# Head norms of a two-block transformer: the sum of squares in two reduced fp32 matmuls in place of one in plain fp32

## The chip, the core and the metric

The kernel runs on one core of one Trainium2 chip. The metric is the device time of one execution in microseconds (us); the time of a version is the median of its runs. Engines: PE is TensorE (matmuls; PEld is its loading of weights), DVE is VectorE, ACT is ScalarE, POOL is GpSimd, SP issues the DMAs.

## What is computed

A sequence of 512 tokens of width 1024 goes through two transformer blocks. The first has a stick-breaking attention, a forgetting attention ("fox") and an attention over 256 memory tokens; the second has a gated delta rule (the GDN stage, 8 heads of width 128), a banded attention and a cross attention. What matters here are the norms over a head:

```python
def rmsnorm(x, g):
    xf = x.astype(jnp.float32)
    y = xf * lax.rsqrt(jnp.mean(xf * xf, axis=-1, keepdims=True) + EPS)
    return (y * g.astype(jnp.float32)).astype(x.dtype)
...
        fq = rmsnorm(to_heads(fx_q, FOX_HEADS, HD), g_fox_q[l])
        fk = rmsnorm(to_heads(fx_k, FOX_HEADS, HD), g_fox_k[l])
...
        mq = rmsnorm(to_heads(m_q, MEM_HEADS, MEM_HD), g_mem_q[l])
        mk = rmsnorm(to_heads(mk, MEM_HEADS, MEM_HD), g_mem_k[l])
...
def _l2norm(x):
    return x * lax.rsqrt(jnp.sum(x * x, axis=-1, keepdims=True) + EPS)
...
    q = _l2norm(_to_chunks(q.astype(f32), A_HEADS, A_DK)) * (A_DK ** -0.5)
    k = _l2norm(_to_chunks(k.astype(f32), A_HEADS, A_DK))
...
        oa = rmsnorm_2(oa, head_norm[l]) * jax.nn.silu(za.reshape(b, s, A_HEADS, A_DV))
```

## The kernel before

Activations lie transposed: 128 features on the partitions, the 512 tokens (256 for the memory) along the row. A projection (`product`, L983) takes 128 output features at a time and eight blocks of 128 input features. Weights and activations are each split into a rounded high part and the rest, so each block costs three matmuls in the reduced fp32 format (f32r in the code, fp32r in the profile): `hh` by `whi` (L995), `hl` by `whi` (L997) and `hh` by `wlo` (L1001). The weights come in units of eight blocks, 512 KB: SP loads a unit into `stage`, ACT rounds it into `whi` (L1413), and DVE (L1778) or POOL (L2238) subtracts to get `wlo`, in stages that `lo_engine` sets. POOL does it in the fox stage and in the GDN stage, DVE in the memory projections.

A norm over a head is four steps of `Schedule.norm` (L384), laid out over several turns of the schedule so that other work lies between them: `hn_sq`, ACT squares the rows (L1478, `norm_square`); then an empty turn; `hn_mm`, PE sums over the features with one plain fp32 matmul against a matrix of ones, or of two blocks of ones for heads of 64 (`head_norm`, L1017, recorded as L950), and ACT takes Ln (L1451) and Exp (L1453) of the sum; `hn_out`, DVE multiplies the rows by it (L1883, recorded as L1781). There are 40 such norms: 4 over the memory keys with 256 columns, 8 for q and k of the fox heads, 4 for the memory queries (these 12 in the fox stage), and in the GDN stage 16 for q and k (`l2q`, `l2k`) and 8 for the output of a head (`oa`), all with 512 columns. The squares of the `oa` norm lie in buffers of the head's cell (`cu`, `cwt`), those of all others in `sqb0`, so an `oa` norm and an `l2k` norm can be under way together.

Each engine works its own list of steps in order, and the list is one order for all: the generators of `Schedule` are mixed (`mix`, `pipe`, `par`), `settle` (L891) sets the banks and what must be free before a step, and each engine's program runs through that one list and issues what is its own. Nothing overtakes on an engine: an instruction that waits holds up all behind it. In the fox stage the projections of the next pair and the norms are interleaved with softmax blocks: DVE finds a maximum (L1932), ACT takes the exponential (L1560, L1575), DVE scales by the sum (L1943, L1958), PE transposes (L953), ACT copies back (L1567, L1582) and PE multiplies by the values. In the GDN stage PE alternates between small 64x64 matmuls that invert a triangle (tiles in `ya`, with DVE between them), the scan of the head before (`cu`, `cs`, `cuu`), and projections of the head after.

The square step on ACT and the matmul of a norm on PE before:

```python
    def norm_square(o):
        wait(o.raw_ref)
        free(o.u_sq)
        act.activation(o.sq, o.raw, ACT.Square).then_inc(*up("hn_sq", o.no))
...
    def head_norm(o):
        pe.wait_ge(*at("hn_sq", o.no))
        free(o.u_bank)
        mm(bank[o.u_bank.bank][:, 0:o.n], o.ones, o.sq, True, True).then_inc(*up("pe_hn", o.no))
```

Of the kernel before, what the change touches and what calls it, by code (L numbers as in the profile page):

```python
# [8 lines left out]
F32 = mybir.dt.float32  # L9
# [7 lines left out]
T = 512  # L17
# [117 lines left out]
class Kernel:  # L135
# [43 lines left out]
    def allocate(self):  # L179
# [3 lines left out]
        self.R = sb("rr", [128, T])  # L183
        self.vecs, self.cft = sb("vecs", [128, NVEC]), sb("cft", [128, NCF])
        self.cbt = sb("cbt", [128, NCB], BF16)
        self.acc = sb("acc", [128, T])
# [23 lines left out]
    def allocate_block1(self):  # L210
# [18 lines left out]
        self.fb = [sb(f"fb{i}", [128, T]) for i in range(4)]  # L229
        self.lf, self.fr, self.lfe = sb("lf", [128, 4, 8]), sb("fr", [128, T]), sb("lfe", [128, 4, 8])  # L230
        self.fxst = [sb(f"fxst{i}", [128, 4]) for i in two]
# [92 lines left out]
class Norm:  # L324
# [13 lines left out]
    u_bank: Use  # L338
    u_out: Use


# [22 lines left out]
class Schedule:  # L364
# [19 lines left out]
    def norm(self, no, out, u_out, raw, raw_ref, ones, scale, gain, n=T, bank="b7", work=None):  # L384
        k = self.k
        sq, r, psq, pr = work or (k.sqb[0][:, 0:n], k.sqb[1][:, 0:n], "sqb0", "sqb1")
        o = Norm(no, out, raw, ones, scale, gain, n, raw_ref, sq, r, Use(psq, [("pe_hn", no)]), Use(pr, [("hn_out", no)]),
                 Use(bank, [("hn_ln", no)]), u_out)
        yield [st("hn_sq", o, o.u_sq)]
        yield []  # L390
        yield [st("hn_mm", o, o.u_bank, o.u_r)]
        yield [st("hn_out", o, *([u_out] if u_out else []))]
# [61 lines left out]
    def mem_kv(self, w, name, raw, nt, mk, mv, gain):  # L454
        items = []
        src = ("mem", w)
        for i in range(2 * nt):
# [8 lines left out]
            elif gain:  # L466
                u = Use(place, [("hn_out", no)])
                g = self.gemm(name, 128 * i, range(8), src, "copy", u, ev, n=NM, out=r[:])
                items.append((g, self.norm(no, mk[:, i, :], None, r[:], ("act_ev", key), self.k.cf("ones"), 1 / 128, self.k.vec(gain), n=NM)))
            else:  # L470
# [49 lines left out]
    def fox_proj(self, p):  # L520
        k, s = self.k, p % 2
        d = self.done2("fox", p)
        pair = k.cf("pair")
        return [self.normed(("fq", p), k.q[s][:], Use(f"q{s}", d), 0, 1536 + 128 * p, pair, 1 / 64, k.vec("g_fox_q")),
# [72 lines left out]
    def block1(self):  # L597
# [14 lines left out]
        def mem_proj(i):  # L612
            return [self.normed(("mq", i), self.mq[i], Use(f"mq{i}", []), i % 2, 3080 + 128 * i, k.cf("ones"), 1 / 128, k.vec("g_mem_q"))]

# [57 lines left out]
    def gdn_proj(self, h):  # L672
# [38 lines left out]
        def unit():  # L711
            yield from silus(*((n, h, k.g3[s][n], ("conv", (n, h))) for n in "qk"))
            for n, g in (("q", 128 ** -0.5), ("k", 1.0)):
                b = k.g3[s][n][:]
                yield from self.norm(("l2" + n, h), b, None, b, ("silu", (n, h)), k.cf("ones"), 1.0, g)

# [40 lines left out]
    def gdn_scan(self, h):  # L757
# [4 lines left out]
        for n in range(8):  # L762
# [4 lines left out]
            if n < 7:  # L767
# [4 lines left out]
        o = k.goT  # L772
        yield from self.norm(("oa", h), o, None, o, ("gc_o", h), k.cf("ones"), 1 / 128, k.vec("head_norm_2"),
                             bank="b6", work=(k.gcell[c]["u"][:], k.gcell[c]["wt"][:], f"cu{c}", f"cwt{c}"))
# [168 lines left out]
def tensor_program(k, pe):  # L943
# [73 lines left out]
    def head_norm(o):  # L1017
        pe.wait_ge(*at("hn_sq", o.no))
        free(o.u_bank)
        mm(bank[o.u_bank.bank][:, 0:o.n], o.ones, o.sq, True, True).then_inc(*up("pe_hn", o.no))  # L1020

# [369 lines left out]
def scalar_program(k, act):  # L1391
# [83 lines left out]
    def norm_square(o):  # L1475
        wait(o.raw_ref)
        free(o.u_sq)
        act.activation(o.sq, o.raw, ACT.Square).then_inc(*up("hn_sq", o.no))  # L1478

    def norm_rsqrt(o):  # L1480
# [197 lines left out]
    for kind, a in k.order:  # L1678
# [10 lines left out]
        elif kind == "tables":  # L1689
            tables()  # L1690
        elif kind == "nsq":
            mem_square(*a)
# [68 lines left out]
def vector_program(k, dve):  # L1761
# [104 lines left out]
    def mem_norm(w, i, gain):  # L1866
# [7 lines left out]
        if i:  # L1874
            hi, lo = (k.mh1, k.mh2)[w - 1]
            dve.wait_ge(*at("sp_hi", (("mem", w), i - 1)))
            tt(lo[:, i - 1, :], tmp[(i - 1) % 2][:], hi[:, i - 1, :].bitcast(F32), ALU.subtract).then_inc(*up("mem_lo", (w, i - 1)))

    def head_norm(o):
# [256 lines left out]
    for kind, a in k.order:  # L2136
# [16 lines left out]
        elif kind == "nout":  # L2153
            mem_norm(*a)
        elif kind == "hn_out":
            head_norm(a)
# [326 lines left out]
```

## Time and profile before

| what | value |
|---|---|
| median of 3 runs | 2376.72 us (2376.33 to 2380.16) |
| the profiled execution, its own time | 2377.33 us |
| its span in the trace | 2375.6 us |
| mean granted TensorE clock over the span | 0.986 |
| instructions in the trace | 32440 |
| busy: DVE, ACT, POOL | 1194.5, 888.9, 432.2 us |

The span is what the trace covers; the profiled execution's own time lies 1.7 us above it. A row of the groups has the line, the engine, the operation, output and inputs by the program's names without buffer numbers, shapes, and a count. A row of the timeline has the start, the duration (of all that are merged into it), the same names, and in brackets how long the engine had been idle before it and what ended that. The end of a matmul is modelled; the distance between the starts of neighbouring matmuls is what the engine really took.

### The profile page before, as it was taken

The page shows a single profiled execution, that of the slowest core. Times are in us where ns is not written, and L with a number is a line of the kernel's source. Part 1 is how long each engine was busy: PE and PEld are TensorE (multiplying, and loading weights), DVE is VectorE, ACT ScalarE, POOL GpSimd, SP SyncE. Part 2 cuts the span into 40 slices and gives each one's busy share as a digit, 9 for nine tenths or more (in the row PEclk, how much of TensorE's full clock was granted, in tenths as well). Part 3 has the DMA queues.
Part 4 walks back from the last instruction along what each step waited for, and adds up shares of the span by engine and source line. Part 5 has one row for each costly group of instructions (what it writes and reads, how often), then busy time and mean ns, then how long its engine had stood idle before and what let it go on. Part 6 is the DMA issues. An engine that isn't in the chain of part 4 may idle for free.

```text
span 2375.6 us, 32440 instructions
## 1 busy us (share of the span) xinstructions
PE 2276.6 (96%) x12924; PEld 1817.5 (77%) x12924; DVE 1194.5 (50%) x1956; ACT 888.9 (37%) x1420; POOL 432.2 (18%) x293
## 2 busy tenths in 40 slices
PE   7999999999999999899999999999999999999997
PEld 5766777888888888677777778777687988888885
DVE  5444454445443444667777522666445445444443
ACT  5444564223322223334333342444434434222222
POOL 1222221001110112434444242000011001101001
PEclk8999999999999999999999999999999999999998
DMA  5213212333333323211121123222133512333332
GB/s 179 80 37 98 63 48 87 90 100 94 98 94 102 98 89 98 86 50 46 56 70 37 36 60 109 81 72 89 54 98 107 157 38 90 98 98 98 98 98 71
DMA packets 58358, 198.94 MB, mean 84 GB/s; under 512 B 6736, under 2 KB 6864, under 8 KB 57952
## 3 DMA queue, kind: packets, MB, share of 16 engines
q1 hardware_dynamic: 58208, 196.86, 26.4%
q8 instruction: 104, 1.70, 0.3%
q14 instruction: 46, 0.38, 0.1%
HBM read 194.67 MB, written 2.16 MB: 83 GB/s over the span
## 4 chain that ended last, share of the span: by engine, by line
PE 50%; DVE 5%; ACT 2%; issue 2%; POOL 1%; DMA 0%; SPq 0%; DVEq 0%; ACTq 0%; POOLq 0%
PE bank L995 14%; PE bank L1001 13%; PE bank L997 13%; PE bank L950 9%; PE bank L953 2%; DVE gv L1781 1%; DVE gq L1781 1%; DVE ya L1778 0%; ACT whi L1413 0%; ACT bdpt L1567 0%; DVE gk L1781 0%; DVE gq L2041 0%; POOL wlo L2238 0%; DVE wlo L1778 0%; ACT cwt L1451 0%
## 5 line engine op out<-in xcount | busy, mean ns | idle before, releaser
L995 PE MATMUL bank<-hh,whi 128*128 128x512 f32 x1680 | 688.3, 410 | 11.5 <-ACT whi L1413 11.5
L1001 PE MATMUL bank<-hh,wlo 128*128 128x512 f32 x1680 | 659.3, 392 | 2.1 <-DVE wlo L1778 1.6
L997 PE MATMUL bank<-hl,whi 128*128 128x512 f32 x1680 | 657.9, 392 | 0.0
L1778 DVE TENSOR_TENSOR wlo<-stage,whi 128x1024 fp32r<-128x1024 f32 x260 | 343.3, 1320 | 295.0 <-ACT whi L1413 294.6
L1413 ACT ACTIVATE whi<-stage 128x1024 fp32r<-128x1024 f32 x340 | 357.4, 1051 | 344.4 <-PE bank L1001 332.5
L995 PEld LDWEIGHTS bank<-hh,whi 128*128 128x128 f32 x1680 | 317.5, 189 | 81.0 <-issue 9.1
L1001 PEld LDWEIGHTS bank<-hh,wlo 128*128 128x128 f32 x1680 | 317.0, 189 | 73.4 <-DVE wlo L1778 3.7
L997 PEld LDWEIGHTS bank<-hl,whi 128*128 128x128 f32 x1680 | 317.9, 189 | 62.8 <-issue 3.6
L2238 POOL TENSOR_TENSOR wlo<-stage,whi 128x1024 fp32r<-128x1024 f32 x80 | 193.9, 2425 | 426.9 <-ACT whi L1413 426.9
L1778 DVE TENSOR_TENSOR x<-bank,x 128x512 f32<-128x512 f32 x80 | 55.3, 692 | 154.2 <-PE bank L1001 154.2
L2238 POOL TENSOR_TENSOR acc<-acc,sqb 128x512 f32<-128x512 f32 x42 | 55.7, 1325 | 325.2 <-ACT sqb L1426 324.6
L995 PE MATMUL bank<-u1h,whi 128*128 128x512 f32 x256 | 99.6, 389 | 0.0
L997 PE MATMUL bank<-u1l,whi 128*128 128x512 f32 x256 | 99.6, 389 | 0.0
L1001 PE MATMUL bank<-u1h,wlo 128*128 128x512 f32 x256 | 99.6, 389 | 0.0
L950 PEld LDWEIGHTS bank<-ya 64*64 64x64 f32 (+1 forms) x2048 | 73.8, 139 | 26.7 <-issue 22.4
L2238 POOL TENSOR_TENSOR u1l<-f1t,u1h 128x512 fp32r<-128x512 f32 x32 | 41.4, 1293 | 265.1 <-ACT u1h L1509 265.1
L950 PE MATMUL bank<-ya 64*64 64x64 f32 (+2 forms) x2048 | 87.3, 231 | 0.0
L2238 POOL TENSOR_TENSOR u2l<-f2s,u2h 128x512 fp32r<-128x512 f32 x22 | 28.5, 1296 | 299.7 <-ACT u2h L1518 299.7
L997 PE MATMUL bank<-u2l,whi 128*128 128x512 f32 x176 | 68.6, 390 | 0.0
L1001 PE MATMUL bank<-u2h,wlo 128*128 128x512 f32 x176 | 68.5, 389 | 0.0
L995 PE MATMUL bank<-u2h,whi 128*128 128x512 f32 x176 | 68.5, 389 | 0.0
L1509 ACT ACTIVATE u1h<-f1t 128x512 fp32r<-128x512 f32 x32 | 20.2, 632 | 126.6 <-DVE f1t L1778 126.6
(363 smaller groups left out, 3471.1 us busy)
## 6 DMA issues: line engine op xcount, KB each, us to landing
stage<-in_wall SPq DMA_DIRECT2D x340, 512.0 KB, 3.5
band<-in_toep SPq DMA_DIRECT2D x16, 256.0 KB, 4.4
x<-in_xT SPq DMA_DIRECT2D x8, 256.0 KB, 5.6
fb<-rowsf SPq DMA_DIRECT2D x8, 256.0 KB, 3.8
gbc<-rows SPq DMA_DIRECT2D x8, 256.0 KB, 3.2
gbc<-rowsc SPq DMA_DIRECT2D x16, 128.0 KB, 3.7
out_y<-fout SPq DMA_DIRECT2D x8, 256.0 KB, 2.2
memx<-in_memT SPq DMA_DIRECT2D x1, 1024.0 KB, 8.8
```

Of the source, the lines that this page charges most:

```text
L950: return pe.matmul(out, w, r, start=start, stop=stop, skip_group_check=True)
L953: return pe.transpose(out, in_, k.cf("ident"))
L995: pe.matmul(o, wh, hi, start=j == 0, stop=False)
L997: pe.matmul(o, wh, lo, start=False, stop=False)
L1001: i = pe.matmul(o, wl, hi, start=False, stop=end)
L1413: act.activation(k.whi[u % NSPLIT][:], k.stage[u % NSTAGE][:], ACT.Copy).then_inc(*up("whi", u))
L1509: act.activation(k.u1[0][:, a["t"] % 16, :], a["b"][:], ACT.Copy).then_inc(*up("sp_hi", ("u1", a["t"])))
L1778: return dve.tensor_tensor(out, a, b, op)
L1781: return dve.scalar_tensor_tensor(out=out, in0=a, scalar=s, in1=b, op0=op0, op1=op1)
L2238: return pool.tensor_tensor(out, a, b, op)
```

## The change

The squares are split like the weights. ACT squares as before, then waits for its own square and copies it, rounded, into `sqh`; DVE subtracts and leaves the rest in `sql`; PE sums both with two matmuls in reduced fp32 into the same bank, against copies of the matrices of ones in that format, which ACT makes once near the start. `sqh` and `sql` exist once: the next norm's copy waits for the second matmul of the norm before (`pe_hn`). The buffer of the plain squares is free once `sql` is written. To make room, the row buffer `fr` of the forgetting attention now lies in `acc`.

```diff
@@ -182,6 +182,8 @@
+        self.sqh, self.sql = sb("sqh", [128, T], F32R), sb("sql", [128, T], F32R)
+        self.onesr = {"ones": sb("onesr", [128, 128], F32R), "pair": sb("pairr", [128, 128], F32R)}
@@ -227,7 +229,7 @@
-        self.lf, self.fr, self.lfe = sb("lf", [128, 4, 8]), sb("fr", [128, T]), sb("lfe", [128, 4, 8])
+        self.lf, self.fr, self.lfe = sb("lf", [128, 4, 8]), self.acc, sb("lfe", [128, 4, 8])
@@ -384,9 +387,9 @@ Schedule.norm
-        o = Norm(no, out, raw, ones, scale, gain, n, raw_ref, sq, r, Use(psq, [("pe_hn", no)]), Use(pr, [("hn_out", no)]),
-                 Use(bank, [("hn_ln", no)]), u_out)
-        yield [st("hn_sq", o, o.u_sq)]
+        o = Norm(no, out, raw, ones, scale, gain, n, raw_ref, sq, r, Use(psq, [("hn_lo", no)]), Use(pr, [("hn_out", no)]),
+                 Use(bank, [("hn_ln", no)]), u_out, Use("sqhl", [("pe_hn", no)]))
+        yield [st("hn_sq", o, o.u_sq, o.u_hl)]
...
@@ -1015,9 +1018,13 @@ PE
     def head_norm(o):
-        pe.wait_ge(*at("hn_sq", o.no))
+        wait(("onesr", 0))
+        pe.wait_ge(*at("hn_hi", o.no))
         free(o.u_bank)
-        mm(bank[o.u_bank.bank][:, 0:o.n], o.ones, o.sq, True, True).then_inc(*up("pe_hn", o.no))
+        out = bank[o.u_bank.bank][:, 0:o.n]
+        mm(out, o.ones, k.sqh[:, 0:o.n], True, False)
+        pe.wait_ge(*at("hn_lo", o.no))
+        mm(out, o.ones, k.sql[:, 0:o.n], False, True).then_inc(*up("pe_hn", o.no))
@@ -1476,6 +1483,14 @@ ACT
         act.activation(o.sq, o.raw, ACT.Square).then_inc(*up("hn_sq", o.no))
+        free(o.u_hl)
+        act.wait_ge(*at("hn_sq", o.no))
+        act.activation(k.sqh[:, 0:o.n], o.sq, ACT.Copy).then_inc(*up("hn_hi", o.no))
+
+    def ones():
+        act.wait_ge(*at("ld_cf", 0))
+        for name, t in k.onesr.items():
+            act.activation(t[:], k.cf(name), ACT.Copy).then_inc(*up("onesr", 0))
@@ -1876,6 +1893,10 @@ DVE
+    def square_lo(o):
+        dve.wait_ge(*at("hn_hi", o.no))
+        tt(k.sql[:, 0:o.n], o.sq, k.sqh[:, 0:o.n].bitcast(F32), ALU.subtract).then_inc(*up("hn_lo", o.no))
```

`square_lo` is issued at the step `hn_sq` of the list, `ones` at the step `consts`, right before the weight units of the memory keys. All norms now take their ones from `k.onesr`.

How the lists of the engines change, at two places. First ACT in the GDN stage, at a head's `oa` norm (squares in `cu`) and the `l2k` norm of the head after (squares of `gk` in `sqb`). Before:

```order
L1453 ACTIVATE sqb<-sqb 128x512 [waits hn_ln]
L1478 ACTIVATE cu<-ya 128x512 [waits gc_u,gc_s,pe_po,gc_o]
L1478 ACTIVATE sqb<-gk 128x512 [waits pe_hn,silu]
L1451 ACTIVATE cwt<-bank,eps 128x512 [waits pe_hn]
L1453 ACTIVATE cwt<-cwt 128x512 [waits hn_ln]
L1451 ACTIVATE sqb<-bank,eps 128x512 [waits pe_hn,hn_out]
```

and of the change:

```order
L1460 ACTIVATE sqb<-sqb 128x512 [waits hn_ln]
L1485 ACTIVATE cu<-ya 128x512 [waits gc_u,gc_s,pe_po,gc_o]
L1488 ACTIVATE sqh<-cu 128x512 [waits hn_sq,pe_hn]
L1485 ACTIVATE sqb<-gk 128x512 [waits hn_lo,silu]
L1488 ACTIVATE sqh<-sqb 128x512 [waits hn_sq,pe_hn]
L1458 ACTIVATE cwt<-bank,eps 128x512 [waits pe_hn]
L1460 ACTIVATE cwt<-cwt 128x512 [waits hn_ln]
L1458 ACTIVATE sqb<-bank,eps 128x512 [waits pe_hn,hn_out]
```

The second copy into `sqh` stands ahead of the Ln of the first norm and waits for PE to be done with the first norm's two matmuls. On DVE at the same place, of the change, with buffer numbers:

```order
L1795 TENSOR_TENSOR ya<-bank3,cft 128x256 [waits pe_P,pe_Y]
L1795 TENSOR_TENSOR sql<-cu1,sqh 128x512 [waits hn_hi]
L1798 SCALAR_TENSOR_TENSOR gq1<-gq1,sqb1 128x512 [waits hn_r]
L1798 SCALAR_TENSOR_TENSOR gz_0<-bank0,rr 128x512 [waits pe_w,gs_oz]
L1795 TENSOR_TENSOR sql<-sqb0,sqh 128x512 [waits hn_hi]
L1795 TENSOR_TENSOR ya<-ya,bank4 128x256 [waits pe_Y]
```

Both subtractions are new; the second stands ahead of the last correction of `ya` that the small matmuls of the inverse wait for. Second DVE in the fox stage, at the norm of q of the fourth pair (`mmst` and `sbW` belong to a memory block, `fxzb`, `fxst` and `sbA` to a fox block). Of the change:

```order
L1971 TENSOR_SCALAR mmst<-mmst 128x2 [waits sm_mx]
L1795 TENSOR_TENSOR sql<-sqb0,sqh 128x512 [waits hn_hi]
L1953 ISA fxzb0,fxst0<-bank2,fb0 128x384 [waits pe_s,sm_n,sm_p]
L1953 ISA fxst0 128x1
L1956 TENSOR_SCALAR fxst0<-fxst0 128x1 [waits sm_mx]
L1953 ISA fxzb1,fxst1<-bank3,fb1 128x384 [waits pe_s,sm_n,sm_p]
L1953 ISA fxst1 128x1
L1956 TENSOR_SCALAR fxst1<-fxst1 128x1 [waits sm_mx]
L1975 RECIPROCAL mmst<-mmst 128x2 [waits sm_p]
L1979 TENSOR_SCALAR sbW0<-sbW0,mmst 128x256 [waits sm_rc]
```

Before, the first row is followed at once by the `fxzb0` row; the subtraction now stands between them.

## Rows read from the trace of the kernel before

**Rows 1.** The page, its first section: the busiest engine

```profile
PE 2276.6 (96%) x12924; PEld 1817.5 (77%) x12924; DVE 1194.5 (50%) x1956; ACT 888.9 (37%) x1420; POOL 432.2 (18%) x293
```

**Rows 2.** Windows: us, PE, PEld, DVE, ACT, POOL busy (count), clock, DMA share, GB/s

```profile
183.00:335.00 152.00, 147.17 (x786) 106.42 (x785) 71.97 (x190) 79.24 (x177) 36.92 (x16) 1.00 0.23 74
955.00:1420.00 465.00, 432.38 (x3988) 338.01 (x3986) 289.67 (x473) 186.78 (x261) 183.75 (x119) 0.98 0.17 54
```

**Rows 3.** Timeline of PE around one norm of the fox stage

```profile
199.16 0.39 PE L1001 MATMUL bank<-hh,wlo 128*128 128x512 f32 x1
199.39 1.02 PE L950 MATMUL bank<-sqb,cft 128*128 128x512 f32 x2
...
200.48 0.40 PE L997 MATMUL bank<-hl,whi 128*128 128x512 f32 x1
```

**Rows 4.** The squares, line L1478: ns min/median/max, first and last start

```profile
L1478 ACT ACTIVATE sqb<-qr x12: 613/616/632, 183.1 to 321.5; 128x512 f32<-128x512 f32 x12
L1478 ACT ACTIVATE sqb<-gq x8: 611/612/617, 971.0 to 1314.3; 128x512 f32<-128x512 f32 x8
...
L1478 ACT ACTIVATE cu<-ya x8: 615/616/631, 1069.0 to 1408.7; 128x512 f32<-128x512 f32 x8
L1478 ACT ACTIVATE sqb<-mraw x4: 402/406/407, 42.5 to 58.4; 128x256 f32<-128x256 f32 x4
```

**Rows 5.** The nearest copies and subtractions, by line and by tile

```profile
L1676 ACT ACTIVATE oah<-ya x8: 613/641/644, 1075.3 to 1416.5; 128x512 fp32r<-128x512 f32 x8
L1778 DVE TENSOR_TENSOR cqd<-gq,ya x8: 678/680/684, 995.2 to 1343.8; 128x512 f32<-128x512 f32 x8
L1778 DVE TENSOR_TENSOR oml<-nm1tmp,omh x8: 412/426/1518, 27.7 to 39.9; 128x256 fp32r<-128x256 f32 x8
L1778 DVE TENSOR_TENSOR sbA<-sbA x16: 292/412/2383, 86.2 to 191.1; 128x128 f32<-128x128 f32 x8, 128x256 f32<-128x256 f32 x8
```

**Rows 6.** Timeline, where the new copies of the ones come in

```profile
42.13 0.58 PE L1001 MATMUL bank<-omh,wlo 128*128 128x256 f32 x1 [0.45 <-DVE wlo L1778]
```

**Rows 7.** Timeline, the second norm of the memory keys

```profile
51.82 0.41 ACT L1478 ACTIVATE sqb<-mraw 128x256 f32<-128x256 f32 x1
...
51.95 1.23 DVE L1778 TENSOR_TENSOR wlo<-stage,whi 128x1024 fp32r<-128x1024 f32 x1 [1.93 <-ACT whi L1413]
...
52.33 0.65 PE L950 MATMUL bank<-sqb,cft 128*128 128x256 f32 x2
...
53.08 0.47 ACT L1451 ACTIVATE sqb<-bank,eps 128x256 f32<-128x256 f32 x1 [0.85 <-PE bank L950]
```

**Rows 8.** Timeline of the fox stage at the norm of q of the fourth pair

```profile
309.45 0.56 DVE L1932 CUSTOM_DVE_ANT_0 fxzb<-bank,fb 128x384 f32<-128x384 f32 x1
...
310.94 0.63 ACT L1478 ACTIVATE sqb<-qr 128x512 f32<-128x512 f32 x1
...
311.13 2.41 POOL L2238 TENSOR_TENSOR wlo<-stage,whi 128x1024 fp32r<-128x1024 f32 x1 [12.54 <-ACT whi L1413]
...
313.84 0.63 PE L953 MATMUL bank<-cft,sbW 128*128 128x128 f32 x4
```

**Rows 9.** Timeline of the GDN stage, a cluster of two norms and what follows

```profile
1119.59 0.62 ACT L1478 ACTIVATE cu<-ya 128x512 f32<-128x512 f32 x1
...
1120.97 1.13 PE L950 MATMUL bank<-cu,cft 128*128 128x512 f32 x2
...
1124.76 1.50 DVE L1781 SCALAR_TENSOR_TENSOR gk<-gk,sqb 128x512 f32<-128x512 f32 x1 [0.49 <-ACT sqb L1453]
...
1126.69 5.39 DVE L1781 SCALAR_TENSOR_TENSOR gv<-cx,vecs,gv 128x512 f32<-128x512 f32 x3
...
1132.46 0.68 PE L950 MATMUL bank<-cft,ya 64*64 64x64 f32 x16 [2.27 <-DVE ya L1778]
```

**Rows 10.** Timeline of PE at the start of the GDN stage

```profile
971.63 2.08 PE L950 MATMUL bank<-sqb,cft 128*128 128x512 f32 x2 [3.06 <-ACT sqb L1478]
...
989.67 0.59 PE L950 MATMUL bank<-cft,ya 64*64 64x64 f32 x6 [4.50 <-DVE ya L1778]
```

More of the change, by code:

```diff
@@ L339 @@
     u_out: Use
+    u_hl: Use
 @dataclass(eq=False)
@@ L468, in mem_kv @@
                 g = self.gemm(name, 128 * i, range(8), src, "copy", u, ev, n=NM, out=r[:])
-                items.append((g, self.norm(no, mk[:, i, :], None, r[:], ("act_ev", key), self.k.cf("ones"), 1 / 128, self.k.vec(gain), n=NM)))
+                items.append((g, self.norm(no, mk[:, i, :], None, r[:], ("act_ev", key), self.k.onesr["ones"][:], 1 / 128, self.k.vec(gain), n=NM)))
             else:
@@ L522, in fox_proj @@
         d = self.done2("fox", p)
-        pair = k.cf("pair")
+        pair = k.onesr["pair"][:]
         return [self.normed(("fq", p), k.q[s][:], Use(f"q{s}", d), 0, 1536 + 128 * p, pair, 1 / 64, k.vec("g_fox_q")),
@@ L612, in mem_proj @@
         def mem_proj(i):
-            return [self.normed(("mq", i), self.mq[i], Use(f"mq{i}", []), i % 2, 3080 + 128 * i, k.cf("ones"), 1 / 128, k.vec("g_mem_q"))]
+            return [self.normed(("mq", i), self.mq[i], Use(f"mq{i}", []), i % 2, 3080 + 128 * i, k.onesr["ones"][:], 1 / 128, k.vec("g_mem_q"))]
         def blocks(a, b):
@@ L714, in unit @@
                 b = k.g3[s][n][:]
-                yield from self.norm(("l2" + n, h), b, None, b, ("silu", (n, h)), k.cf("ones"), 1.0, g)
+                yield from self.norm(("l2" + n, h), b, None, b, ("silu", (n, h)), k.onesr["ones"][:], 1.0, g)
         def chain():
@@ L772, in gdn_scan @@
         o = k.goT
-        yield from self.norm(("oa", h), o, None, o, ("gc_o", h), k.cf("ones"), 1 / 128, k.vec("head_norm_2"),
+        yield from self.norm(("oa", h), o, None, o, ("gc_o", h), k.onesr["ones"][:], 1 / 128, k.vec("head_norm_2"),
                              bank="b6", work=(k.gcell[c]["u"][:], k.gcell[c]["wt"][:], f"cu{c}", f"cwt{c}"))
@@ L1690, in scalar_program @@
             tables()
+        elif kind == "consts":
+            ones()
         elif kind == "nsq":
@@ L2154, in vector_program @@
             mem_norm(*a)
+        elif kind == "hn_sq":
+            square_lo(a)
         elif kind == "hn_out":
```

## The prediction, written before the change was run

> **What bounds the kernel now.** I read the page first: PE is busy 96% of the span, 2276.6 of 2375.6 us [rows 1]. So PE time that is taken away is time saved, unless PE then waits. The windows say where it already waits: in the fox stage it is idle 4.8 of 152 us, in the GDN stage 32.6 of 465 us [rows 2]. The timelines at the norms decide the rest. For each of the 40 norms I asked three things: when does ACT end the square, when does PE come to the norm's matmul, and what do DVE and POOL do in between. The new work lies exactly in that gap.
>
> **What PE saves.** Matmuls of a projection start about 0.23 us apart. From the L1001 at 199.16 to the L997 at 200.48 lie 1.32 us, in which PE does that L1001, the norm and one L995: two normal steps of 0.23 leave 0.86 us for the plain fp32 matmul, recorded as two passes [rows 3]. Two matmuls in reduced fp32 are two normal steps, 0.46 us. That is 0.40 us saved for each of the 36 norms with 512 columns (12 + 8 + 8, and 8 more of `gk` that look like those of `gq`) [rows 4], and about 0.2 for the 4 with 256. All of it together: 36 x 0.40 + 4 x 0.2 = 15.2 us. This is the most that can be won.
>
> **What is added on the way from square to sum.** Before, the path was the square alone. Now it is: a copy on ACT, 0.64 us by the copy `oah<-ya`; a subtraction on DVE, 0.68 us by `cqd<-gq,ya`, 0.43 for 256 columns by `oml` [rows 5]. PE can issue the second matmul about 1.4 us after the square ends if DVE is free and in turn. Two things make it later. DVE works in order, so the subtraction waits for what stands before it and holds what stands behind. And it reads two operands from SBUF: subtractions of that sort (`sbA<-sbA`) usually take 0.3 to 0.4 us but up to 2.38 us [rows 5], and the three `gv` multiplications took 5.39 us while POOL was busy, where three of 0.7 would be 2.1 [rows 9]. I read this as follows: such an instruction of DVE doesn't move while POOL's runs, and ends some 0.55 us after it.
> The Trainium skill says the same in SBUF — State Buffer, section "Who interferes with whom": a DVE instruction with two SBUF inputs and a GpSimd instruction that reads SBUF exclude each other for the whole instruction. By that rule the fox term below is what I give; without it the subtraction there would end 1.2 us earlier and the sum would be about 2.4 us lower.
>
> **Ones.** Two copies of 128x128 on ACT stand right before a weight split that PE is already waiting for through DVE's `wlo` [rows 6]. No row shows that size; between 0 and two of the 0.64 us for four times the columns, I take 0.25 each, as half the size of the 0.4 us operations with 256 columns (estimate): **+0.5**, bounds 0 and 1.3.
>
> **Memory keys, 4 norms.** The first has 4 us of room and what follows waits for something else: 0. In the other three the square (51.82 to 52.23) ends as PE arrives at 52.33. The copy ends near 52.63, but DVE is in `wlo` until 53.18 and the subtraction stands behind it: 53.2 to 53.63, second matmul at 53.7. Before, the passes ended 0.65 us after their start and the Ln came 0.1 later, at 53.08; a single cheaper matmul ends some 0.28 after its start (estimate), so the Ln comes near 54.08 [rows 7]. Ln, Exp, the eviction, the weight split and the next square follow each other on ACT without a gap, so the 1.0 us doesn't come back: 3 x 1.0 = **+3.0** (bounds 2.4 and 3.6).
>
> **Fox stage, 12 norms.** The slack between square and PE is 2.7 to 6.4 us, so the matmul itself is in time everywhere, even with POOL's 2.4 us in the way: 12 x -0.40 = -4.8. But the subtraction also delays the softmax chain behind it on DVE. In eight of the twelve PE doesn't need that chain soon. The dearest is the q norm of the fourth pair: DVE did the maximum `fxzb` at 309.45, before the square (310.94 to 311.57). Now the subtraction stands in front and waits for the copy (312.2), then for POOL (until 313.54), and ends at 314.1. The two maxima (0.56 and, by my estimate, 0.15 for their small operations), and a reciprocal with a scaling (0.5 together, estimate) come after: `sbW` is ready at 316.1 where PE wanted it at 313.84 [rows 8]: +2.3. Three more places of the same kind, with less of a delay, give by the same working 0.4, 0.9 and 0.8, and one more costs the 0.4 that it saves. Sum: -4.8 + 2.3 + 2.1 + 0.4 = **0.0**, bounds -4.8 (the chain has slack I don't see) and +4.
>
> **GDN stage, 24 norms.** At the start PE waits 3.06 us for the square and then does the fp32 matmul at the low level of the clock in 2.08 us [rows 10]; the copy and subtraction add 1.35, the cheaper matmuls take about that much off: 0. Its k norm saves 0.4 ahead of a wait of 4.5 us on DVE [rows 10]: 0. The next two norms (second head): -0.4 and -0.1. Then six times the cluster of rows 9. The q norm ahead of it saves 0.4, and all that follows starts 0.4 earlier: square of `oa` at 19.19 (+1100), copy to 20.45, subtraction 20.55 to 21.24, second matmul near 21.4, its sum known at 21.85. Only then the second copy may overwrite `sqh`: to 22.47. DVE meanwhile has `gq` and `gz` behind the first subtraction, 0.68 each as in rows 5, and is free at 22.6; second subtraction to 23.3, second matmul 23.4. So the Exp of the k norm ends, and `gk` can start, at 25.2 instead of 24.76: +0.45. PE's inverse starts near 23.8, 0.9 later than before. But neither sets the pace: PE stands 2.27 us at 1132.46 waiting for DVE, and DVE is held by alternating with POOL in the `gv` multiplications (5.39 us) [rows 9]. POOL's chain starts only 0.15 to 0.2 later, so I take +0.2 a head, net of what the q norm saves; the bounds are -0.4 (all hidden) and +0.9 (PE's delay passes through). 6 x 0.2 = +1.2. The last two `oa` norms: -0.4 and, where the weight split stands behind the copy, +0.6. Sum of the stage: **+0.9**, bounds -2.7 and +5.1.
>
> **Sum:** 0.5 + 3.0 + 0.0 + 0.9 = **+4.4 us**, on the profiled execution's own 2377.33 us: 2381.7. The median of the runs is 0.6 us lower than that execution; what I left at nothing (ACT's extra 0.64 us in front of exponentials, 12 times in the fox stage) can only add. I forecast **2382 us**: PE's saving of 15 us is real, and is spent on waits for the new chain. About 0.2% (4.8 us) is what a measurement can tell from no change, and the forecast lies on that edge.
>
> **The rivals.**
> 1. *The waits are covered* (faster). Where DVE's delay meets slack in both softmax and inverse, the fox stage gives -4.8 and the GDN stage -2.7: with 3.5 for the start that is -4.0, or 2373, just inside the bound; each us that the memory keys hide as well takes it below, down to -15.2 or 2362. For it: the slack of 3 us and more at most norms, PE's share of 96%. Against it: rows 7, where nothing lies between square and matmul. Chance 0.13 for over 0.2% faster.
> 2. *One buffer for two norms* (slower). `sqh` is shared, so at the six clusters the second norm can't start before the first is summed, and DVE holds the subtraction in front of the correction of `ya` that PE's inverse needs. If that delay of 0.9 us passes through instead of vanishing in the wait of 2.27 us, it is +4.2 over my sum; with the fox stage at its upper bound, +4. Then 2386 to 2390. It decides as soon as PE's wait at rows 9 is used up, or POOL's chain moves by as much as ACT's. Chance 0.43 for over 0.2% slower, the upper half of my own range included.
> 3. *The matmuls don't get cheaper*: were each of the two to cost what half the plain one does, 0.43, nothing would be saved and the time would be 2397. The projections' step of 0.23 us in the same format speaks against it; 0.02, inside the chance of slower.
>
> **How the numbers follow.** The forecast's own neighbourhood, 2373 to 2381.5, has 0.44 (same), rival 1 has 0.13 (faster), the rest 0.43 (slower). The range takes in the bounds of the fox and GDN stages, which I don't expect to fall on the same side both: 2372 to 2391.
>
> **What would show it.** In the profile after: the pair of matmuls 0.46 us apart from start to the next projection where they don't wait; in the memory keys a wait of PE for DVE's `sql` of about 1 us, three times; near 313.8 a wait of PE for `sbW` of 2 us; DVE rows `sql` of up to 3 us in the fox stage where POOL runs; at a cluster a wait of about 0.4 us before each second matmul, and the distance between clusters, 50.6 us before (from 1069.0 [rows 4] to 1119.59 [rows 9]), at 50.8. It would be wrong if the distance is under 50.3 or over 51.4, or if the stretch from 183 to 335 gets shorter by more than 3 us.

## The result and the profile after

| | before | after |
|---|---|---|
| median | 2376.39 us (2375.06 to 2380.16, 12 runs) | 2382.76 us (2376.44 to 2384.6, 12 runs) |
| span of the profiled execution | 2375.6 us | 2382.8 us |
| mean granted clock over it | 0.986 | 0.983 |

The ratio of after to before is 1.002 with the interval [1.001, 1.0029]: slower by 6.4 us. The forecast was 2382, so the number was right. Two things were missing from its reasons, the granted clock in the fox stage and what ACT's copy does in front of an exponential, and the first of them is what most of the experiments are about. The profiled execution of the changed kernel is the slowest of its twelve runs (2384.60 us); three of the twelve took 2376.4 to 2377.1 us, at a mean clock of 0.986 to 0.987.

The page after, its first section, and below the dots the new groups from the list of all groups by shape (busy us and mean ns, then idle time before them and what ended it):

```profile
PE 2275.8 (96%) x12924; PEld 1823.4 (77%) x12924; DVE 1220.8 (51%) x1996; ACT 913.2 (38%) x1462; POOL 435.8 (18%) x293
...
L1795 DVE TENSOR_TENSOR sql<-sqb,sqh 128x512 fp32r<-128x512 f32 x28 | 29.3, 1048 | 23.1 <-ACT sqh L1488 22.5
L1488 ACT ACTIVATE sqh<-sqb 128x512 fp32r<-128x512 f32 x28 | 17.7, 631 | 6.8 <-PE bank L953 4.8
L953 PE MATMUL bank<-sql,onesr 128*128 128x512 f32 x28 | 13.2, 471 | 3.3 <-DVE sql L1795 3.3
L953 PE MATMUL bank<-sqh,onesr 128*128 128x512 f32 x28 | 13.1, 469 | 8.1 <-ACT sqh L1488 8.1
```

Against [rows 1], PE's busy time is the same within 1 us although the plain fp32 passes are gone; DVE has 26 us more and ACT 24 us more. A part of PE's saving must have gone back into PE being slower, and the windows say where (us, PE, PEld, DVE, ACT, POOL busy, clock, DMA share, GB/s):

```profile
183.00:335.00 152.00, 142.79 (x747) 104.58 (x746) 82.87 (x198) 83.61 (x183) 36.00 (x15) 0.98 0.23 74
955.00:1420.00 465.00, 430.26 (x3991) 340.86 (x3990) 302.89 (x504) 198.90 (x285) 186.91 (x118) 0.97 0.18 55
```

In the fox stage the clock was 1.00 before [rows 2] and is 0.98 now, and PE idles 9.2 us where it idled 4.8. The 4.4 us more lie at four places: 2.3 at the fourth pair, 0.9, 0.6 and 0.6 at three others. The squares, ns min/median/max and first and last start, give the stages' limits:

```profile
L1485 ACT ACTIVATE sqb<-qr x12: 612/616/643, 186.0 to 327.3; 128x512 f32<-128x512 f32 x12
L1485 ACT ACTIVATE sqb<-gq x8: 611/613/616, 977.1 to 1321.5; 128x512 f32<-128x512 f32 x8
```

Against [rows 4] the first fox square is 2.9 us later, the twelfth 5.8, the first of the GDN stage 6.1, and the end of the span 7.3. So the start has cost 2.9, from there to the GDN stage another 3.2, and the rest 1.2: 0.8 from the first square of the GDN stage to the last `oa` square in it, 0.4 behind that.

### Where the time went, place by place

**A norm where nothing waits** (timeline of PE in the fox stage):

```profile
201.68 0.39 PE L1004 MATMUL bank<-hh,wlo 128*128 128x512 f32 x1
201.91 0.39 PE L953 MATMUL bank<-sqh,pairr 128*128 128x512 f32 x1
202.14 0.39 PE L953 MATMUL bank<-sql,pairr 128*128 128x512 f32 x1
202.36 0.39 PE L998 MATMUL bank<-hh,whi 128*128 128x512 f32 x1
```

The pair takes 0.45 us from its first start to the next projection, where plain fp32 took 0.86 [rows 3]. The saving of 0.40 is there.

**The memory keys** (timeline, the second norm, as [rows 7]):

```profile
52.27 0.41 ACT L1485 ACTIVATE sqb<-mraw 128x256 f32<-128x256 f32 x1
...
52.41 1.23 DVE L1795 TENSOR_TENSOR wlo<-stage,whi 128x1024 fp32r<-128x1024 f32 x1 [1.94 <-ACT whi L1420]
...
52.77 0.42 ACT L1488 ACTIVATE sqh<-sqb 128x256 fp32r<-128x256 f32 x1
...
53.24 0.38 PE L953 MATMUL bank<-sqh,onesr 128*128 128x256 f32 x1 [0.30 <-ACT sqh L1488]
53.55 0.42 DVE L1795 TENSOR_TENSOR sql<-sqb,sqh 128x256 fp32r<-128x256 f32 x1
...
54.02 0.39 PE L953 MATMUL bank<-sql,onesr 128*128 128x256 f32 x1 [0.40 <-DVE sql L1795]
...
54.51 0.47 ACT L1458 ACTIVATE sqb<-bank,eps 128x256 f32<-128x256 f32 x1 [1.32 <-PE bank L953]
```

From square to Ln it is 2.24 us, where it was 1.26 [rows 7]: 0.98 for each of three norms, in the order that was predicted (DVE's `wlo` first, then the subtraction).

**The q norm of the fourth pair** (timeline, as [rows 8]):

```profile
313.24 0.63 ACT L1485 ACTIVATE sqb<-qr 128x512 f32<-128x512 f32 x1
...
313.43 2.40 POOL L2261 TENSOR_TENSOR wlo<-stage,whi 128x1024 fp32r<-128x1024 f32 x1 [12.14 <-ACT whi L1420]
...
314.63 1.75 DVE L1795 TENSOR_TENSOR sql<-sqb,sqh 128x512 fp32r<-128x512 f32 x1 [2.86 <-ACT sqh L1488]
...
316.30 0.55 DVE L1953 CUSTOM_DVE_ANT_0 fxzb<-bank,fb 128x384 f32<-128x384 f32 x1
...
317.90 0.61 DVE L1979 TENSOR_SCALAR sbW<-sbW,mmst 128x256 f32<-128x256 f32 x2
...
318.40 0.63 PE L956 MATMUL bank<-cft,sbW 128*128 128x128 f32 x4 [2.41 <-DVE sbW L1979]
```

POOL ends at 315.83 and the subtraction at 316.38, 0.55 later; the maximum comes behind both, and PE stands 2.41 us. The transposes are at 318.40 instead of 313.84, 4.56 later, of which 2.30 was there already at the square (313.24 for 310.94): the place cost 2.26 us. The same operation takes 0.69 us where POOL is still, as at the clusters below. The Trainium skill, SBUF — State Buffer, section "Who interferes with whom", says that a DVE instruction with two SBUF inputs contends with a GpSimd instruction that reads SBUF, and calls the ports that they share "an exclusive lock". This agrees with it, but for the 0.14 us by which the 0.55 is shorter than a whole subtraction.

**What was not predicted** follows right behind. Four windows of PE (us, PE busy, clock, DMA share, GB/s):

```profile
276.00:282.20 6.20, 4.48 (x33) 1.00 0.64 208
282.20:285.60 3.40, 3.40 (x10) 0.50 0.20 83
314.00:319.70 5.70, 3.29 (x17) 1.00 0.32 92
319.70:323.10 3.40, 3.40 (x10) 0.51 0.00 0
```

Twice PE idles (1.7 us in the first window, 2.4 us in the third, each time for a scaling on DVE that stands behind `sql`), and right after it the granted clock is at its low level, 1.2 GHz, with PE busy throughout. The second wait is new. Of the first, 1.14 us was there before, with the clock full behind it; what lengthened it is shown with the run `latefox`. A third wait, of 1.59 us at 301.98, is as long as before and has the full clock behind it. Matmuls of a projection then start 0.43 us apart instead of 0.23:

```profile
283.08 0.63 PE L1004 MATMUL bank<-hh,wlo 128*128 128x512 f32 x1
283.50 0.63 PE L998 MATMUL bank<-hh,whi 128*128 128x512 f32 x1
```

Eight matmuls in 3.4 us, each 0.20 late, are 1.6 us lost, twice. The Trainium skill, TensorE: Matmul & The Clock Gate, section "What's actually happening", says that "the default state is throttled, and activity releases the throttle"; that the fall comes right after PE's two longest waits agrees with it.

**A cluster of the GDN stage** (timeline, as [rows 9]; its start is 6.38 us later than there):

```profile
1125.97 0.61 ACT L1485 ACTIVATE cu<-ya 128x512 f32<-128x512 f32 x1
...
1127.33 0.69 DVE L1795 TENSOR_TENSOR sql<-cu,sqh 128x512 fp32r<-128x512 f32 x1 [1.57 <-ACT sqh L1488]
...
1128.08 0.50 PE L953 MATMUL bank<-sql,onesr 128*128 128x512 f32 x1 [0.23 <-DVE sql L1795]
...
1128.62 0.63 ACT L1488 ACTIVATE sqh<-sqb 128x512 fp32r<-128x512 f32 x1 [0.80 <-PE bank L953]
...
1129.31 0.50 PE L953 MATMUL bank<-sqh,onesr 128*128 128x512 f32 x1 [0.72 <-ACT sqh L1488]
...
1130.46 2.13 PE L953 MATMUL bank<-ya 64*64 64x128 f32 x32
...
1132.01 1.24 DVE L1798 SCALAR_TENSOR_TENSOR gk<-gk,sqb 128x512 f32<-128x512 f32 x1 [0.73 <-ACT sqb L1460]
...
1133.68 5.24 DVE L1798 SCALAR_TENSOR_TENSOR gv<-cx,vecs,gv 128x512 f32<-128x512 f32 x3
...
1139.31 0.68 PE L953 MATMUL bank<-cft,ya 64*64 64x64 f32 x16 [1.55 <-DVE ya L1795]
```

The second copy waits 0.80 us for the shared `sqh`, and PE 0.72 for it. The three `gv` multiplications begin 7.71 us after the square, where it was 7.10 [rows 9], and take 5.24 instead of 5.39. From the square to the last row it is 13.34 us, where it was 12.87: 0.47 more; the cheaper q norm between clusters gives 0.40 back, and the distance between this cluster and the one before is 50.69 (50.63 before).

### The profile page after: what moved, and what is told of

Read it like the earlier page. It is cut to its first block, busy times and chain, and to the rows that moved or that the text cites. A ratio compares the mean times of both kernels' runs of the same rounds, so it can differ in the third digit from the quotient of the medians.

```text
span 2382.8 us, 32561 instructions
## 1 busy us (share of the span) xinstructions
PE 2275.8 (96%) x12924; PEld 1823.4 (77%) x12924; DVE 1220.8 (51%) x1996; ACT 913.2 (38%) x1462; POOL 435.8 (18%) x293
## 4 chain that ended last, share of the span: by engine, by line
PE 50%; DVE 5%; ACT 3%; issue 2%; POOL 1%; DMA 0%; SPq 0%; ACTq 0%; DVEq 0%; POOLq 0%
PE bank L998 14%; PE bank L1004 13%; PE bank L1000 13%; PE bank L953 8%; PE bank L956 2%; DVE gv L1798 1%; DVE gq L1798 1%; DVE sql L1795 0%; DVE ya L1795 0%; ACT whi L1420 0%; ACT sqh L1488 0%; ACT sqb L1458 0%; ACT bdpt L1582 0%; DVE gk L1798 0%; DVE gq L2062 0%
```

## The experiments

All twelve start from the changed kernel. "Fox" is the time from the first fox square to the first of the GDN stage in the profiled execution, in brackets how much of it was at the low clock; "cluster" is the distance between two `oa` squares where the clock is full in between (several such distances of one profile agree within 0.05, but for one of 50.97 after the change and one of 50.71 in `gdn_plain`); "at 0.985" is the time that a straight line through a kernel's runs (time over their mean granted clock) gives for a clock of 0.985. The kernel before has there 94 runs, that fall by 1.3 us for each 0.001 of clock; the other lines fall by 0.9 to 2.1. With so few runs the last column is uncertain by 0.3 to 0.8 us (one standard error), for `best4` by 1.4; `best4` and `no_lo` have no run at 0.985, so theirs are extrapolations.

| | median (range, runs) | ratio to before | fox | cluster | mean clock | at 0.985 |
|---|---|---|---|---|---|---|
| before | 2376.39 (2375.06–2380.16, 12) | | 787.8 (0) | 50.63 | 0.9876 | 2378.4 |
| after | 2382.76 (2376.44–2384.6, 12) | [1.001, 1.0029] | 791.1 (6.8) | 50.70 | 0.9838 | 2379.6 |
| mem_plain | 2378.87 (2375.76–2384.74, 10) | [1.0009, 1.0029] | 789.2 (3.4) | 50.70 | 0.9833 | 2376.5 |
| fox_plain | 2376.70 (2375.57–2381.66, 10) | [1.0002, 1.002] | 787.6 (0) | 50.70 | 0.9855 | 2378.4 |
| gdn_plain | 2380.45 (2379.07–2383.57, 6) | [1.0017, 1.0042] | 791.1 (6.8) | 50.62 | 0.9857 | 2381.5 |
| no_lo | 2371.56 (2369.22–2374.58, 10) | [0.9975, 0.9994] | 780.8 (0) | 49.91 | 0.9818 | 2367.6 |
| latefox | 2377.76 (2373.74–2379.69, 12) | [1.0001, 1.0019] | 786.1 (3.4) | 50.71 | 0.9844 | 2376.0 |
| two | 2381.07 (2377.94–2383.4, 7) | [1.0013, 1.0034] | 789.3 (3.4) | 50.25 | 0.9829 | 2378.5 |
| early | 2378.12 (2373.54–2379.44, 11) | [1.0004, 1.0021] | 789.5 (3.4) | 50.70 | 0.9845 | 2377.0 |
| best | 2375.05 (2369.65–2378.63, 11) | [0.9993, 1.001] | 786.5 (3.4) | 50.70 | 0.9840 | 2374.1 |
| best2 | 2374.07 (2368.25–2377.7, 11) | [0.9986, 1.0004] | 785.0 (0) | 50.25 | 0.9836 | 2371.8 |
| best4 | 2367.68 (2364.25–2369.2, 5) | [0.9955, 0.998] | 785.0 (0) | 50.18 | 0.9890 | 2371.2 |
| foxonly | 2373.09 (2371.18–2377.23, 11) | [0.9986, 1.0004] | 784.9 (0) | 50.62 | 0.9864 | 2375.6 |
| late | 2379.75 (2373.42–2381.54, 11) | [1.0003, 1.0021] | 785.0 (0) | 50.68 | 0.9836 | 2377.2 |

The runs of before beside the first four kernels had a median of 2375.67, beside the next four 2375.46, then 2374.87 for three, and 2376.04 for the last; the first eight ran on one chip, the next three and the last on two others.

### One part back in plain fp32, and the low half left out

The three parts differ in one line, here with the name of its run behind it; norms with `plain` take one fp32 matmul of the squares and neither copy nor subtraction:

```diff
+        plain = no[1] == "mkv"                      # mem_plain
+        plain = no[0] in ("fq", "fk", "mq")         # fox_plain
+        plain = no[0] in ("l2q", "l2k", "oa")       # gdn_plain
...
+        if o.plain:
+            pe.wait_ge(*at("hn_sq", o.no))
+            free(o.u_bank)
+            mm(bank[o.u_bank.bank][:, 0:o.n], o.ones, o.sq, True, True).then_inc(*up("pe_hn", o.no))
+            return
```

> The change, with the 4 norms of the memory keys back at one plain fp32 matmul (no copy, no subtraction there). Theory (waits for the new chain): the 3.0 us of the memory keys go, the first square of the fox stage starts at 183.1 to 183.7 instead of 186.0, the rest keeps its shifts; about 2379.7 us by median of the change 2382.8. Rival (the low clock in the fox stage is the whole loss): the time stays within 1 us of the change, since the fox stage is untouched.

The median, 2378.87, is 3.9 us under the changed kernel, so the rival falls. The first fox square came 0.13 us after that of the kernel before, instead of 2.90. From the first memory norm on, where the profiles stood 0.3 apart, this is 0.42: the ones. The three norms are the other 2.5. At the same clock the kernel is 3.1 us under the changed one.

> The change, with the 12 norms of the fox stage back at plain fp32. Theory (DVE's order, POOL and the waits, with the clock falling after them): no stretch at the low clock between 183 and 335 us, no growth of the shift over the stage (before to change it grew by 3.2 us, from 2.9 at 186.0 to 6.1 at 977.1), about 2379.6 us, and the scatter of the runs (2376.4 to 2384.6 with the change) shrinks to 2 or 3 us. Rival (ACT's added copies are the cost, wherever they stand): 12 of 40 copies less, 30% of the loss, about 2381 us.

Fox 787.6, as before the change, with the clock full and no growth of the shift. Two parts of the expectation missed: the median is 2376.70, 3 us under what the theory gave, and the runs still scatter over 6.1 us. The median is 6 us under the changed kernel, the value at the same clock 1.2 (uncertain by 0.7). So the fox norms cost little work and much clock.

> The change, with the 24 norms of the GDN stage back at plain fp32. Theory: the stage cost about 1 us in all (shift 6.1 at its first square, 6.9 at its last), so about 2381.8 us, the distance between clusters back from 50.69 to 50.64. Rival (the shared sqh at six clusters is the main loss, 0.9 us each): 5 us less, about 2377.5 us. Rival (ACT's copies): 60% of the loss goes, about 2379 us.

The fox stage repeats the changed kernel's, both stretches at the low clock included. The interval of the ratio overlaps with that of the changed kernel, so the median doesn't tell the theory from no effect; the rivals' 2377.5 and 2379 lie under all six runs. The clusters tell more: with plain GDN norms the distances at the full clock are 50.61 to 50.65 in three kernels (one of 50.71), with the split ones and the shared buffer 50.66 to 50.73 in seven (one of 50.97). The split costs a cluster 0.07.

The fourth leaves the low half of the squares out (no subtraction, one matmul):

```diff
-        mm(out, o.ones, k.sqh[:, 0:o.n], True, False)
-        pe.wait_ge(*at("hn_lo", o.no))
-        mm(out, o.ones, k.sql[:, 0:o.n], False, True).then_inc(*up("pe_hn", o.no))
+        mm(out, o.ones, k.sqh[:, 0:o.n], True, True).then_inc(*up("pe_hn", o.no))
```

> The change without the low half: ACT's copy and the one reduced matmul on it stay, DVE's subtraction and the second matmul are gone, so the sum is of the rounded squares alone. Theory (DVE's part of the chain is the cost): memory keys cost 0 to 0.4 each, the fox stage gains 12 x 0.63 = 7.6 us, the GDN stage 0 to 8 (at the clusters the second copy still waits), together 2362 to 2371 us, no low clock in the fox stage. Rival (ACT's copies are the cost): 2380 us or more.

Fox 780.8 at the full clock, 7.0 under before where 7.6 was expected, with ACT's copies still in place: taken over the stage, the copies in front of the exponentials cost little. The median, 2371.56, is 0.6 over the top of the theory's range. Its clock is the lowest of all, 0.9818: of the 10.8 us that it gains at equal clock 4.1 are left in the medians (2375.67 beside it).

### The subtraction one turn later in the fox stage

```diff
         yield [st("hn_sq", o, o.u_sq, o.u_hl)]
-        yield []
+        yield [st("hn_lo", o)] if no[0] in ("fq", "fk", "mq") else []
...
-        elif kind == "hn_sq":
+        elif kind == "hn_lo" or kind == "hn_sq" and a.no[0] not in ("fq", "fk", "mq"):
             square_lo(a)
```

> The fox stage alone: DVE's subtraction of these 12 norms is issued one turn of the schedule later, behind a maximum or a scaling of the softmax that it stood ahead of. If the loss of the fox stage comes from the softmax chain that waits on DVE behind the subtraction (theory), then the sbW scaling of the fourth pair is on time, the granted clock doesn't fall in the stretch from 183 to 335 us, the shift of the twelfth square against the kernel before goes from +5.7 down to about +1 to +2, and the time is 2376 to 2379. If ACT's copy in front of the exponentials is the cost (rival), the shift stays near +5.7 and the time near 2382. If the two stretches at the low clock are chance (second rival), they come back in other places and the time lies anywhere between.

Shift of the twelfth square +1.4, fox 786.1, 4.9 less than after the change, median 2377.76: for the stage as a whole the theory holds and the rival of the copy falls. Of the 4.9 some 1.7 is one stretch at the low clock less, as a comparison of kernels shows: with the early subtraction the stage takes 791.1 with two stretches and 789.2 to 789.5 with one, with the late one 786.1 to 786.5 with one and 784.9 to 785.0 with none. The order itself is worth the other 3. At the fourth pair (timelines of DVE and PE) the maxima are done ahead of the subtraction, and PE waits 1.00 instead of 2.41 us (0.15 before the change):

```profile
313.29 1.75 DVE L1795 TENSOR_TENSOR sql<-sqb,sqh 128x512 fp32r<-128x512 f32 x1 [1.37 <-ACT sqh L1488]
...
315.15 0.62 DVE L1979 TENSOR_SCALAR sbW<-sbW,mmst 128x256 f32<-128x256 f32 x2
```

```profile
315.65 0.63 PE L956 MATMUL bank<-cft,sbW 128*128 128x128 f32 x4 [1.00 <-DVE sbW L1979]
```

The stretch at the low clock near 282 stayed in this profile, against the theory's word that none would. So did most of the wait ahead of it (timelines of PE, first before, then `latefox`, then `no_lo`):

```profile
279.49 1.03 PE L953 MATMUL bank<-cft,sbA 128*128 128x128 f32 x5 [1.14 <-DVE sbA L1943]
```

```profile
280.06 1.14 PE L956 MATMUL bank<-cft,sbA 128*128 128x128 f32 x6 [1.64 <-DVE sbA L1964]
```

```profile
275.46 1.25 PE L956 MATMUL bank<-cft,sbA 128*128 128x128 f32 x7 [1.65 <-DVE sbA L1962]
```

In `latefox` no subtraction stands ahead of this scaling, and `no_lo` has none at all; with the fox norms plain it is 0.92. What is left is ACT's copy: in `latefox` the square starts at 277.22, the copy at 277.95 and the first exponential that the scaling needs at 278.49, 1.27 after the square; before it was 0.52 after it (277.39 and 277.91). At this one place the rival is right, and the copy costs 0.5 us.

Over all kernels, one profile each: the five with the early subtraction (after, `mem_plain`, `gdn_plain`, `two`, `early`) have waits of 1.7 to 2.0 and of 2.4 us at these two places, and the low clock followed 7 of the 10. The six with the late one have 1.64 and 1.0, and it followed 2 of the 12, both times the longer. The kernel before, `fox_plain` and `no_lo` have 0.9 to 1.7 and at most 0.3, and it followed none of the 6. The wait of 1.6 us near 300 has the full clock behind it in all fourteen. So the low clock follows PE's longer waits, but not strictly; what else decides is not shown.

### A rounded half of their own for the oa norms

```diff
+        self.sqh2 = sb("sqh2", [128, T], F32R)
...
-                 Use(bank, [("hn_ln", no)]), u_out, Use("sqhl", [("pe_hn", no)]))
+                 Use(bank, [("hn_ln", no)]), u_out, Use("sqh2" if work else "sqhl", [("pe_hn", no)]), Use("sql", [("pe_hn", no)]))
```

> The oa norms get a rounded half of their own (sqh2); the rest is shared as before. Theory (DVE and POOL alternating over gv set the pace of a head): the wait of 0.8 us of the second copy at a cluster goes, but the distance between clusters, 50.69 us after the change, falls by at most 0.1 to 0.2, and the time by 1 us at most: 2381 to 2383. Rival (the shared buffer passes its delay through): the distance falls by 0.5 or more, 6 times, and the time is 2379 or less.

The distance fell by 0.45 to 50.25: the theory's number is refuted, and the rival's 0.5 is nearly reached. Timeline of a cluster at the full clock, whose square is at 1125.35:

```profile
1127.23 0.63 ACT L1496 ACTIVATE sqh<-sqb 128x512 fp32r<-128x512 f32 x1
...
1127.92 0.50 PE L958 MATMUL bank<-sqh,onesr 128*128 128x512 f32 x1
...
1132.62 5.25 DVE L1809 SCALAR_TENSOR_TENSOR gv<-cx,vecs,gv 128x512 f32<-128x512 f32 x3
...
1138.26 0.68 PE L958 MATMUL bank<-cft,ya 64*64 64x64 f32 x16 [1.27 <-DVE ya L1806]
```

The copy's wait is gone. The three `gv` multiplications still alternate with POOL and take 5.25 us, but they begin 7.27 us after the square instead of 7.71, and all behind them comes 0.43 to 0.45 earlier. So the alternation does stand on the path, as the theory had it; its error was that the wait for the buffer would vanish ahead of it. Only in the clusters of this profile with a stretch at the low clock do the three take 2.3 us (0.75 each), since POOL comes only at their end; those distances are 52.0. The time came down by 1.7 only, with intervals that overlap: five distances of 0.45 are 2.3, and the mean clock was lower again.

### The start repaired, and all together

`early` has plain memory keys and makes the ones at the step `consts_in`, behind them. `best` is that with the late fox subtraction; `best2` adds the buffer of `two`; `best4` has every subtraction late, in the GDN stage too; `foxonly` is `best` with plain GDN norms; `late` is the changed kernel with every subtraction late and nothing else.

```diff
-        elif kind == "consts":
+        elif kind == "consts_in":
             ones()
```

> The memory keys in plain fp32 as before, and the two copies of the ones made where ACT still has room, behind the memory keys, instead of in front of their weight units. Theory (the start costs 0.45 for the ones and 2.9 for the three norms): the first square of the fox stage stands within 0.1 us of the kernel before and the time is 3.4 us under the changed kernel at the same clock: 2378 to 2379.5, or 0.4 to 0.5 under the kernel with the plain memory keys alone. Rival (the granted clock of the rest of the program gives the saving back, as it partly did in the run with the plain memory keys): the shift at the fox stage is 0 but the end is at 2380 to 2383.

2378.12, in the theory's range; the first fox square 1.13 us ahead of the kernel before, not level with it: from the first memory norm on it is 0.6, and here the low clock at the start lasted 10.2 us instead of 13.7. In `best`, with the same start, the low clock reaches as far past the first memory norm as before (3.7 and 3.6 us, against 2.5 in `early`), and the time from there to the first fox square is 140.62 us where it was 140.61: level, as the theory had it.

> Memory keys plain, ones late, and the subtraction of the fox norms one turn later, all together. If the terms add (theory): 0 at the first square of the fox stage, -2 to -4 at its end, +0.9 in the GDN stage, so 2373 to 2376, faster than the changed kernel by 7 us or more and not slower than the kernel before. If the fox stage is held by something else than the order on DVE (rival): as the kernel with the start repaired alone, 2378 to 2379.5.

2375.05, 7.7 us under the changed kernel and the same as before: in the median the terms add. In its profile the fox stage gave 1.3 us, with one stretch at the low clock in it, where 2 to 4 were expected.

> As the run with the start repaired and the fox subtraction late, and with a rounded half of their own for the oa norms. In the run with that buffer alone the distance between clusters at the full clock was 50.25 us where the shared one has 50.70. If the terms add (theory): distance 50.2 to 50.3, about 2.5 us off the GDN stage, time 2372 to 2373.5, below both kernels. If the granted clock gives it back (rival): the distances at the full clock are as said, but more stretches at the low clock, and the time stays at 2374.5 to 2376.

The cluster and the fox stage are as said (50.25; 785.0 at full clock), the median between the two expectations, 2374.07, and not clear of the kernel before (the interval reaches 1.0004). At the same clock it is 2.3 us under `best`.

> As the last, and DVE's subtraction one turn later in the GDN stage too, where it then stands behind the scaling of gq and behind the last correction of ya that PE's inverse waits for. Theory (DVE and POOL alternating over gv set the pace, and the subtraction stood in front of ya): distance between clusters at the full clock 49.8 to 50.2, time 2370 to 2373. Rival (the k norm of the cluster is the later one, and it now ends later): distance 50.3 to 51.0, time 2373 to 2376.

2367.68, faster than both kernels, by 7.2 us against before (ratio 0.9968). But the distance is only 0.07 under `best2`'s, near the upper end of what the theory gave, while the time is 2.3 us under its range. Most of the 6.4 us to `best2` goes with the clock, 0.9890 against 0.9836: at 0.985 the two are 0.6 apart, less than the uncertainty of 1.4. With five runs, all between 0.987 and 0.991, it stays open whether this order makes the clock higher or these runs had luck.

> Only the 12 norms of the fox stage split, with the late subtraction; memory keys and GDN stage in plain fp32. Theory (fox term with the late subtraction -3.3 at the full clock and -1.7 with one stretch at the low clock in it; GDN term of the split with the shared buffer within 0.5 us of nothing): 2373 to 2375.5, as the kernel with all but the memory keys split, and distance between clusters 50.63 again. Rival (the split of the GDN norms costs the 0.9 us or more that the prediction gave): 1 to 3 us below that kernel's 2375.05, so 2372 to 2374.

2373.09 lies in the range of the theory and in that of the rival, so the time doesn't tell them apart; the distances are back at 50.62, as the theory had it. Against `best`, on another chip, the split of the 24 GDN norms comes out as 1.5 us gained at the same clock (uncertain by 0.6), and the mean clock is 0.9840 instead of 0.9864, which at 1.3 us for each 0.001 costs 3.1.

> The changed kernel with one thing moved: every subtraction of DVE one turn later, in the GDN stage too; start, shared buffer and all else as the change has them. Theory (the order on DVE is most of the loss, and the low clock follows PE's waits): fox stage as in the run with the late fox subtraction, -1.7 to -3.3; distance between clusters at the full clock 50.2 to 50.7; fewer stretches at the low clock in the GDN stage than with the early subtraction, and 2372 to 2376. Rival (the second oa buffer was what gave the last kernel its 6 us under the one with the early subtraction in the GDN stage): time as with the late fox subtraction alone, 2376.5 to 2379.

A miss for both: the fox stage is as said (785.0), but the clusters stay at 50.68 and the profile has 27.3 us at the low clock among them where after the change it had 13.7. 2379.75, 2 us over `latefox`. With the shared buffer the late subtraction wins nothing in the GDN stage: the `gv` multiplications begin 7.7 us after the square, as after the change.

## Why the prediction was right, and where not

- *Matmuls*: 0.86 read before, 0.46 predicted for the pair and 0.45 measured. Rival 3 is out.
- *Ones* +0.5: 0.42 (two copies of 0.29 us).
- *Memory keys* +3.0: 0.98 a norm at the place, as predicted; 2.5 in all by the run with plain keys, since some 0.5 is made up before the first fox square.
- *Fox stage* 0.0: **this term failed, it measured +3.2**. Its work was right: at the dearest place 2.3 predicted, 2.26 measured; the blocked subtraction ended 0.55 after POOL; over all places 4.8 predicted against 4.4 of new waits. (The working counts eight places without a cost and five with one, of twelve norms; one is counted twice.) Missing was a term for the granted clock. Two of PE's waits, one new and one longer than before, were followed by stretches at 1.2 GHz, 1.6 us each by the matmuls' steps; without them 791.05 - 3.2 = 787.85, which is the 787.84 of before. The kernels with one stretch less (789.2 to 789.5) give 1.5 to 1.9 for one. The runs with the late subtraction show the other side: with the wait at the fourth pair at 1.0, the stage is 785.0 at the full clock. ACT's copy in front of the exponentials, left at nothing in the sum, costs 0.5 us at one place, and the low clock followed just that wait in `latefox` and `best`.
- *GDN stage* +0.9: 0.8 in the profile, from its first square to its last. The second copy ends 3.28 us after the square of a cluster, `gk` starts 6.04 after it, where 3.28 and 6.01 were predicted, and the `gv` multiplications and POOL's first operation begin 0.6 later after the square, net of the q norm 0.2, where 0.15 to 0.2 was predicted for POOL. The distance grew by 0.07 instead of 0.2, since the `gv` multiplications got 0.15 shorter. The last distance is 0.44 shorter and the one before it 0.58 longer, where -0.4 and +0.6 were predicted. Single terms agree better than the total can show: one stretch at the low clock does more than the whole term (a distance of 52.09 with one, 50.70 without). *Rival 2*, one buffer for two norms, was rated at what passes through beyond the sum; the buffer does cost 0.45 a cluster, as the run `two` shows, but inside the sum, where the q norm's gain covers it.
- *The whole*: 2382 predicted, 2382.76 measured. Start 0.6 too dear, fox stage 3.2 too cheap. That the number fits so well is in part luck. The sum of 4.4 stands against 7.3 in the profile, and the forecast was saved by the profiled execution being the slowest of twelve, 1.8 us over the median. By the lines through the runs the change costs 1.2 us at the same clock (uncertain by 0.6); its mean clock is 0.9838 instead of 0.9876, and that goes with the other 5. The profile without its two fox stretches gives 4.1. Which of the two is nearer to the cost of the work stays open, since the mean clock sums up the whole program, and the waits that the change makes are part of what moves it.

Of the checks named in advance, the pair's 0.46, the wait for `sbW` (2.41 for 2) and the cluster (50.70 for 50.8) came as said; in the memory keys PE waits 0.40 for `sql` and 0.30 for `sqh`, where about 1 for `sql` was said; `sql` took at most 1.8 us instead of 3, and PE waits 0.23 before the second matmul instead of 0.4, but 0.72 before the second norm's first.

## What to carry to other kernels

Price a cheaper instruction by what its operands need: here 0.40 us saved on PE asked for a copy and a subtraction on two engines that work in order, and where the subtraction stood in the list was worth 3 us of waits in the fox stage, and 1.1 to 1.9 more for each stretch at the low clock that went with them. A new step goes behind what another engine is about to need, one buffer per norm under way, and stays out of places with no slack. And on a kernel bound by PE, look at the granted clock before and after waits are added: a wait of 2 us can cost its own length and then a slow stretch.

## What the runs showed of the hardware

- The same kernel scatters with the clock that it is granted: of the 94 runs of before, the 24 at 0.990 took 2371.3 to 2372.7 us and the 39 at 0.987 took 2374.4 to 2377.4. Comparing medians alone mixes this with the work.
- A gain in work can be taken back by the clock: the kernels with split GDN norms had 0.9829 to 0.9855 (`best4` apart), those with plain ones 0.9857 to 0.9876, and `no_lo`, with the least work on PE, 0.9818. Why is not shown. Less work on PE alone doesn't explain it, since `best4` has the same instructions as `best2` in another order, and 0.9890 against 0.9836.
- What a stretch at the low clock costs is not in proportion to its length: for most clusters 1.3 to 1.8 us, whether it lasted 3.4 or 6.8 us, for three of 10.2 us 2.9 to 3.6, and in `early` and `best` one of 3.4 us cost nothing (50.3 against 50.7). The mean clock of a span is therefore only a rough price.
